# First turn of the expert weights: the pieces behind the prefill as whole 4 MB transfers

## What is computed

```
g = min(xb @ w_gate[e] + b_gate[e], 7);  u = clip(xb @ w_up[e] + b_up[e], -7, 7)
out = (g * sigmoid(1.702 * g) * (u + 1)) @ w_down[e] + b_down[e]
y[rows] += out * weight
```

## Time and profile before

| | |
|---|---|
| median of three runs | 1230.99 us (1229.31 to 1231.14) |
| profiled execution, its own time | 1230.71 us |
| its span (first to last instruction) | 1228.9 us |
| TensorE busy | 94% of the span |
| granted TensorE clock | 0.999 |
| moved by DMA | 458.59 MB, 373 GB/s over the span |
| 4096 KB weight transfers, median from issue to landing | 32.5 to 35.1 us |

### The profile page before, as it was taken

One profiled execution on the slowest core, in us unless ns is written; L12 is line 12 of the kernel. 1 busy time (PEld: TensorE's weight loads), 2 busy tenths in 40 slices (PEclk: granted clock), 3 DMA queues, 4 the chain that ended last, 5 costly groups with the idle time before them and its releaser, 6 DMA issues.

```text
span 1228.9 us, 13742 instructions
## 1 busy us (share of the span) xinstructions
PE 1160.3 (94%) x5460; PEld 586.8 (48%) x5460; DVE 446.5 (36%) x775; ACT 249.7 (20%) x409; POOL 47.6 (4%) x72
## 2 busy tenths in 40 slices
PE   8999999999999999999999899989999989899998
PEld 5888888787343443434343333424343424343433
DVE  4878798765312131231312131212222121212122
ACT  5555577632110100010010001000110000010000
POOL 2222100200000000000000000000000000000000
PEclk9999999999999999999999999999999999999999
DMA  9454545487999999999999999999999999999994
GB/s 374 146 197 171 189 154 206 169 341 305 429 422 428 428 431 429 437 428 429 438 430 428 434 434 428 430 437 430 428 433 434 429 429 434 434 425 436 434 423 189
DMA packets 28143, 458.59 MB, mean 373 GB/s; under 512 B 3216, under 2 KB 4112, under 8 KB 6608
## 3 DMA queue, kind: packets, MB, share of 16 engines
q1 hardware_dynamic: 26720, 454.14, 87.7%
q0 software_dynamic: 1104, 3.93, 1.0%
q10 hardware_dynamic: 288, 0.10, 0.0%
HBM read 457.11 MB, written 1.05 MB: 373 GB/s over the span
## 4 chain that ended last, share of the span: by engine, by line
PE 66%; DMA 27%; DVE 4%; ACT 1%; issue 1%; POOL 0%; SPq 0%; DVEq 0%; POOLq 0%
PE bank L1712 26%; DMA experts_ring<-in_w_up 25%; PE bank L1423 16%; PE bank L1754 11%; PE bank L1700 4%; PE bank L1640 3%; DMA back<-in_mixer_halves 2%; PE bank L1718 2%; PE bank L1387 1%; DVE back_split L913 1%; PE bank L1719 1%; DVE region L1337 1%; ACT region L891 0%; ACT region L896 0%; ACT back_split L653 0%
## 5 line engine op out<-in xcount | busy, mean ns | idle before, releaser
L1712 PE MATMUL bank<-experts_ring,region 128*64 128x512 f32 x2048 | 455.1, 597 | 28.2 <-DMA experts_ring<-in_w_up 14.4
L1712 PEld LDWEIGHTS bank<-experts_ring,region 128*64 128x64 f32 x2048 | 148.3, 137 | 312.1 <-issue 290.2
L1754 PE MATMUL bank<-experts_ring,region 128*64 128x512 f32 x1024 | 226.8, 595 | 14.3 <-ACT region L891 14.3
L1423 PE MATMUL bank<-back_split,region_split 128*128 128x512 f32 x600 | 176.6, 396 | 0.2
L1754 PEld LDWEIGHTS bank<-experts_ring,region 128*64 128x64 f32 x1024 | 75.6, 137 | 143.1 <-issue 129.1
L1423 PEld LDWEIGHTS bank<-back_split,region_split 128*128 128x128 f32 x600 | 110.5, 188 | 25.1 <-issue 2.0
L1372 DVE COPY region<-bank 64x512 f32<-64x512 f32 x32 | 22.2, 694 | 227.3 <-PE bank L1754 227.3
L913 DVE TENSOR_TENSOR back_split<-back,back_split 128x2048 fp32r<-128x2048 f32 x34 | 77.9, 2291 | 32.4 <-ACT back_split L653 32.2
L1423 PE MATMUL bank<-back_split,front_split 128*128 128x512 f32 x216 | 84.4, 391 | 0.0
L1361 DVE TENSOR_SCALAR region<-bank 128x512 f32<-128x512 f32 x32 | 22.1, 691 | 163.4 <-PE bank L1719 163.4
L884 ACT ACTIVATE region<-region 128x512 f32<-128x512 f32 x32 | 20.1, 630 | 292.0 <-DVE region L1354 292.0
(11 more groups left out here) (174 smaller groups left out, 790.1 us busy)
## 6 DMA issues: line engine op xcount, KB each, us to landing
experts_ring<-in_w_gate SPq DMA_DIRECT2D x26, 4096.0 KB, 32.5
experts_ring<-in_w_up SPq DMA_DIRECT2D x22, 4096.0 KB, 33.9
experts_ring<-in_w_down SPq DMA_DIRECT2D x20, 4096.0 KB, 35.1
experts_ring<-in_w_down SPq DMA_DIRECT2D x24, 2048.0 KB, 21.4
experts_ring<-in_w_up SPq DMA_DIRECT2D x20, 2048.0 KB, 16.0
back<-in_mixer_halves SPq DMA_DIRECT2D x36, 1024.0 KB, 4.8
experts_ring<-in_w_gate SPq DMA_DIRECT2D x12, 2048.0 KB, 12.3
front<-in_mixer_halves SPq DMA_DIRECT2D x8, 1024.0 KB, 4.8
```

The lines of the kernel that those rows point to most:

```text
L1423: ins = nc.tensor.matmul(UB[u % 3][:, :], a[:, k, toks], b[:, cols], start=(k == 0 and m == 0), stop=(k == k_n - 1 and m == 2))
L1712: ins = nc.tensor.matmul(dst[h * SLOTS:(h + 1) * SLOTS, :], XE[:, kk, e * SLOTS:(e + 1) * SLOTS], w[:, k, h * HALF:(h + 1) * HALF], start= ...
L1754: ins = nc.tensor.matmul(bank[2][h * SLOTS:(h + 1) * SLOTS, :], AHT[:, k, half * SLOTS:(half + 1) * SLOTS], w[:, k, h * HALF:(h + 1) * HAL ...
```

## The change

The 27 halves behind the prefill (g = 9 to 35) are no longer issued one by one. g = 9 is still a half by itself, since the other half of its piece, g = 8, belongs to the prefill. From piece 5 on the first turn uses `stream`, as the later turns do: pieces 5 to 12 and 14 to 17 (12 pieces, 24 halves) are transfers of 4 MB that wait for both of their places, and piece 13 stays two halves. TensorE waits once for each whole piece, before its first half; the separate waits for second halves stay for the prefill's pieces 0 to 3, and, by the branch above them, where a second half lies at place 0.

```diff
             elif place(g) == 0:
                 pe.wait_ge(second_in[RING - 1], landed(r, d, n))
-            elif n < PER_TURN // 2:
-                pe.wait_ge(second_in[place(g - 1)], 16 * whole_starts[:n + 1].count(place(g - 1)))
+            elif n < RING // 2:
+                pe.wait_ge(second_in[place(g - 1)], 16)
...
-            for g in range(RING, PER_TURN):
-                sp.wait_ge(used, g + 1 - RING)
-                load_half(g // PER_PAIR, g)
+            sp.wait_ge(used, 1)
+            load_half(0, RING)
+            for n in range(RING // 2 + 1, PER_TURN // 2):
+                stream(n // (PER_PAIR // 2), n, 0)
             later_turns(0)
```

## The result

The changed kernel takes 1233.44 us (median of 14 runs), the kernel before 1230.33 us in the runs beside it. The ratio is 1.0025, with a 95% interval of 1.0017 to 1.0033: 3.1 us slower. The forecast was +2.6 us, with the chance of slower by over 0.2% at 0.51. The profiled execution has a span of 1231.8 us, 2.9 us more.

What follows compares the result with a forecast made beforehand. The prediction took the never-idle DMA queue as the bound. Restart gaps less savings gave +1.6 to +4.1 us, taken as +2.6 on a span of 1228.9: 1231.5 of span, 1233.6 us on the median's level, range 1231.0 to 1235.4.

Steps and rivals of the forecast that it cites:

- The bound: DMA queue without a gap since 310 us: each microsecond idle in the first turn moves the end by the same.
- The moved issues: Pieces 5 to 8 are issued when their second halves were: 323.1, 335.3, 343.0 and 354.7 us.
- The start-up: Time from issue to start of data on an empty queue, at pieces 5 and 6: 2.3 to 4.8, taken as 3.3 us.
- half 2's case: Half 2, taken as alone in the queue, landed 7.2 us after issue: 2.3 us start-up, the lower bound.
- half 13's: Half 13, issued before half 12 landed, seemed to begin its data 4.8 us after issue: the upper bound.
- What came back behind it: After piece 8, the eight whole pieces left in the first turn save 0.065 us each, 0.5 us.
- The saving per whole piece: On the DMA engines, one whole 4 MB transfer is 0.065 us cheaper than two halves; 0.8 us for 12.
- TensorE's lead: Piece 6, first read at 366.7 us, lands by 349.8, 17 us ahead; no wait before the lead is used up.
- a single transfer starts its data within about 1 us: Rival at 335 us, half 13: no gap, 1.2 and 0.8 us come back, 1229.0 us; chance 0.08.
- the lateness is made up later: Rival: something other than the DMA queue bounds the late stage; time stays 1231.0 or falls to 1230.2; chance 0.05.
- fewer transfers save their fixed cost: Rival: each of 12 removed transfers had 2.3 us in the queue's time; 28 us go, 1203 left; chance 0.01.
- the fourth rival: An additional gap at piece 8 or a second TensorE wait; 2.5 us more gives 1236.5; chance 0.03.

Runs made afterwards that it cites:

- piece 6 held back further: Changed kernel with one more wait ahead of piece 6, until seven halves are read; ratio 1.0081 to the kernel before.
- late halves: Changed kernel, but from piece 5 on both halves are issued together as 2 MB transfers when both places are free; ratio 1.0031 to the kernel before.
- only 5 and 6: Kernel before with only pieces 5 and 6 of the first turn as whole transfers, the others as halves; ratio 1.003 to the kernel before.
- only 5: Kernel before with only piece 5 of the first turn as a whole transfer; ratio 1.0009 to the kernel before.
- only 6: Kernel before with only piece 6 of the first turn as a whole transfer; ratio 1.0028 to the kernel before.
- more waits: Changed kernel with 48 more TensorE waits on a semaphore long raised, in the middle of the mixer; ratio 1.0019 to the kernel before.

## Why the prediction was right

- **The bound.** DMA idle time at 310 to 345 us moves the landing at 1173.6 and the end by as much: confirmed by the landing, 2.86 us later with a span 2.9 longer, and by piece 6 held back further.
- **The moved issues.** Predicted 323.1, 335.3, 343.0 and 354.7 us; measured 323.4, 335.5, 343.2 and 354.9. TensorE's reading is unchanged, 0.24 us later from the start. Confirmed.
- **The start-up** was taken as 3.3 us for both restarts, between bounds of 2.3 and 4.8. It measured 2.4 and 4.6 us. Piece 6 alone decides, so its landing is at the upper bound, 349.8, and the lateness at piece 8 is 4.7 us, against a predicted 2.1 to 4.6 and about 3.1 by the value chosen. This is the term that was mis-sized, by 1.6 us of lateness. "The queue is empty at both restarts, which is half 2's case rather than half 13's" was the wrong reason, and both cases were misread. Half 2 was not alone: a transfer of the mixer, issued at 270.1 us, landed at 274.8, after half 2's issue. The half issued at 301.2 did find the queue empty and took 7.4 us, 2.5 besides its data, so the lower bound was right by luck. Half 13 was queued behind half 12 and had no start-up of its own: the first of its 16 updates came 4.9 us behind half 12's first, the last 6.1 behind half 12's last, with a fetch at 337.3. What piece 6 has in common with it is a last share held back beside a fetch.
- **What came back behind it** was predicted as 0.5 us and measured 2.1: the last half of the turn lands at 454.2 before, and the last piece at 456.8 in the changed kernel, 2.6 us later. So 1.6 us were saved that no step of the prediction had. The rows of half 29 of the kernel before, and of pieces 14 and 17 of the changed one:

```profile
L463 SPq DMA_DIRECT2D experts_ring<-in_w_gate x1: 328/328/328, 409.6 to 409.6; - x1
...
DMA to landing us min/median/max: 15.2/15.2/15.2
```

```profile
L467 SPq DMA_DIRECT2D experts_ring<-in_w_gate x1: 327/327/327, 409.8 to 409.8; - x1
...
DMA to landing us min/median/max: 17.8/17.8/17.8
...
L467 SPq DMA_DIRECT2D experts_ring<-in_w_down x1: 328/328/328, 433.1 to 433.1; - x1
...
DMA to landing us min/median/max: 23.7/23.7/23.7
```

  Before, halves 28 and 29 took 424.8 - 413.5 = 11.3 us where two halves take 9.8. In the changed kernel piece 14 follows half 27 (landed at 417.9) in 9.7. An instruction fetch falls at 418 to 419 us in both. In the kernel before it was half 28 that slipped, and only the last of its 16 updates: that came 6.6 us behind half 27's last, the other 15 kept their 4.9. In the changed kernel neither the first, the fifteenth nor the last update moved. It seems that the fetch met the latest share in the one and an earlier one in the other; the profile does not show which. The five other profiled executions with halves there (late halves, only 5 and 6, only 5, only 6 twice) have no such slip at half 28, so this 1.5 us, most of the 1.6, belongs to the one execution of the kernel before. The sum of 2.6 us was thus right by luck, by two errors of 1.6 us that cancel.
- **The saving per whole piece**, 0.065 us, is borne out by the spacing of 9.7 in the changed kernel, but never by a time of its own.
- **TensorE's lead.** Piece 6 landed 17 us before it was read, as predicted. There was no wait for the ring before 500 us.
- **The rivals.** That a single transfer starts its data within about 1 us held by its words: piece 5's and piece 6's first packets began 0.96 us after the issue. But the landing came 2.4 and 4.6 us later than issue plus data, and no time came back, so the rival fell; its condition should have been on the landing. That the lateness is made up later fell with piece 6 held back. That fewer transfers save their fixed cost fell with the late halves: with 12 transfers more the ratio is 1.0031 and not 1.0025, which is 0.7 us, not 28. In the fourth rival the forecast of 1233.6 plus 2.5 us is 1236.1, not 1236.5. The fixed cost of about 2.0 us that the Trainium skill gives for transfers issued by GpSimd (DMA: Bandwidth & Descriptors, Anatomy of one DMA) is near the starts of 2.4 us on an empty queue, and not near those of up to 4.6.

## What to carry to other kernels

Where one queue never rests from some point on, its idle time anywhere behind that point costs the end in full, even hundreds of microseconds before anybody waits for it, and a consumer's lead doesn't help: here piece 6 issued 8.8 us later put the last landing 8.1 us later. Before merging transfers into larger ones, ask when the last of their buffers comes free, and put that beside the time at which the queue runs out of work: whole pieces cost nothing where 4.3 us or more of data were still to land at their issue (piece 8 in the third execution of the changed kernel, 9.7 us behind piece 7), and cost time where 1.3 us or less were (1.4 us at piece 5, 4.7 at piece 6). Between, there is one case: piece 8 with more waits, issued with 2.6 us to go, had 15 of its 16 shares in step. Restarts of a dry queue do not add up; the last of them sets the lateness, and each change ahead of it moves the next one.

## What the runs showed of the hardware

A landing is as late as the latest of its 16 shares, and the shares drift apart in a full queue: 1.5 us between first and last at half 9 of the kernel before, 3.9 at the end of the first turn.

The drift comes in slips, and these go with instruction fetches. The profile counts 20 fetches of 16 KB among the packets of the 16 DMA engines, one every 21 to 30 us in the first turn; with 48 more waits in TensorE's stream the one at 314.8 us came 3.2 us earlier, so they are TensorE's. In the 14 profiled executions, over the 1434 ring transfers issued from 326 to 1170 us, the last of the 16 updates slipped by over 0.8 us nine times while the first kept its step. All nine had such a fetch in their time, and only 118 of the 1434 had one at all. A slip was 0.9 to 1.7 us, and it can stay: at 1173.6 us in the kernel before the last update is still 1.9 us behind the fifteenth. Slips of this size are also the scatter between single profiles here: the last landing differs by 0.4 us between three executions of the changed kernel, and by 1.7 us between two of the kernel with only piece 6 whole, the later of which also had the lower clock described next.

In five of the 14 executions, that of the late halves among them, TensorE's granted clock fell to its lower level, 1.2 GHz, for 3.4 us at 304 to 305 us, and in the kernel with more waits for 10 us. Before it fell, TensorE had run the router's small matmuls with gaps between them; the kernel before had the same matmuls with the same gaps and kept the clock. The window shows the mean of both levels, 0.66, where it is 1.00 in the eight executions that kept it:

```profile
304.00:309.00 5.00, 4.89 (x28) 0.66 0.99 423
```

The ring is then read first at 313.1 us and not at 311.8. A kernel whose queue restarts at TensorE's pace passes such a delay on to the end: half 12 of the late halves was issued 1.3 us after the changed kernel's piece 6, and the restart began there. That one which keeps its queue filled does not pass it on is to be expected, but the kernel before was not profiled with such a drop, so it is not shown.
